# Prompt attention on one core: the values product of each head pair in eleven small groups instead of five

## What is computed

```python
k_nope = einsum('bsc,chd->bshd', c_kv, w_a_uk)
v = einsum('bsc,chd->bshd', c_kv, w_a_uv)
# for each block of 128 queries:
sc = (einsum('bqhd,bkhd->bhqk', qn_b, k_nope)
      + einsum('bqhd,bkd->bhqk', qr_b, k_r)) * ATTN_SCALE
sc = where(k_pos <= q_pos, sc, -inf)          # causal
p = softmax(sc, axis=-1)
o = einsum('bhqk,bkhd->bqhd', p, v)           # 16 heads, 64 values each
```

## Time and profile before

| | |
|---|---|
| median of 3 runs | 1721.11 us (1720.89 to 1722.8) |
| profiled execution | 1720.89 us, its span in the trace 1719.1 us |
| PE busy over the span | 1622.7 us (94%), 10281 matmuls |
| DVE busy | 950.2 us (55%) |
| ACT busy | 570.0 us (33%) |
| POOL busy | 200.1 us (12%) |
| `attend`, 136 to 521 us | PE busy 374.57 of 385 us at a granted clock of 1.00 |

### The profile page before, as it was taken

One profiled execution on the slowest core, in us unless ns is written; L12 is line 12 of the kernel. 1 busy time (PEld: TensorE's weight loads), 2 busy tenths in 40 slices (PEclk: granted clock), 3 DMA queues, 4 the chain that ended last, 5 costly groups with the idle time before them and its releaser, 6 DMA issues. The chain is left out here.

```text
span 1719.1 us, 29475 instructions
## 1 busy us (share of the span) xinstructions
PE 1622.7 (94%) x10281; PEld 1422.9 (83%) x10281; DVE 950.2 (55%) x1855; ACT 570.0 (33%) x1249; POOL 200.1 (12%) x292
## 2 busy tenths in 40 slices
PE   6989999999998999996997999999999999999995
PEld 6978888888885555554877999999999999999984
DVE  4556666656664445544554655456446554464469
ACT  4436555556552232323213311312212113122131
POOL 1000000000000000000341220211202202112001
PEclk9989999999998999996998999999999999999998
DMA  5211111011005656515102211101201111011003
GB/s 157 67 50 30 27 24 24 13 26 27 14 2 157 195 171 175 172 41 183 37 28 86 62 37 47 57 19 61 61 24 61 33 47 57 22 61 49 1 25 111
DMA packets 149343, 109.18 MB, mean 64 GB/s; under 512 B 54791, under 2 KB 137925, under 8 KB 149112
## 3 DMA queue, kind: packets, MB, share of 16 engines
q1 hardware_dynamic: 147848, 105.96, 21.3%
q0 software_dynamic: 816, 1.40, 0.4%
q10 hardware_dynamic: 576, 0.52, 0.1%
HBM read 101.88 MB, written 10.14 MB: 65 GB/s over the span
## 5 line engine op out<-in xcount | busy, mean ns | idle before, releaser
L1683 PE MATMUL banks<-act_hi,up_hi 128*128 128x352 f32 (+2 forms) x1056 | 341.8, 324 | 3.6 <-DVE up_lo L1921 3.6
L1684 PE MATMUL banks<-act_lo,up_hi 128*128 128x352 f32 (+2 forms) x1056 | 339.8, 322 | 0.0
L1685 PE MATMUL banks<-act_hi,up_lo 128*128 128x352 f32 (+2 forms) x1056 | 339.7, 322 | 0.0
L1683 PEld LDWEIGHTS banks<-act_hi,up_hi 128*128 128x128 f32 x1056 | 199.1, 189 | 3.7 <-ACT up_hi L1890 3.7
L1684 PEld LDWEIGHTS banks<-act_lo,up_hi 128*128 128x128 f32 x1056 | 199.3, 189 | 0.0
L1685 PEld LDWEIGHTS banks<-act_hi,up_lo 128*128 128x128 f32 x1056 | 199.0, 188 | 0.0
L1683 PE MATMUL banks<-gated_hi,down_hi 128*128 128x352 f32 (+2 forms) x528 | 172.0, 326 | 3.4 <-DVE o_t L2025 2.5
L1952 DVE TENSOR_TENSOR o_t<-o_t,banks 128x352 f32<-128x352 f32 x240 | 121.0, 520 | 93.8 <-PE banks L1685 93.5
L1931 DVE SCALAR_TENSOR_TENSOR conv_out<-conv_in,conv_now,conv_out 128x1072 f32<-128x1072 f32 x42 | 65.1, 1550 | 190.6 <-ACT conv_out L1831 190.6
L1684 PE MATMUL banks<-gated_lo,down_hi 128*128 128x352 f32 (+2 forms) x528 | 169.8, 322 | 0.0
L1685 PE MATMUL banks<-gated_hi,down_lo 128*128 128x352 f32 (+2 forms) x528 | 169.5, 321 | 0.0
(11 more groups left out here) (269 smaller groups left out, 3110.1 us busy)
## 6 DMA issues: line engine op xcount, KB each, us to landing
c_stage<-in_cache_kv_latent SPq DMA_DIRECT2D x252, 128.0 KB, 2.2
weight_stage<-in_w_f_up SPq DMA_DIRECT2D x44, 512.0 KB, 4.5
down_stage<-in_w_f_down SPq DMA_DIRECT2D x22, 512.0 KB, 4.3
o_t<-in_x_prompt SPq DMA_DIRECT2D x8, 512.0 KB, 3.8
rope_rows<-in_cache_k_rope SPq DMA_DIRECT2D x256, 16.0 KB, 2.0
r_stage<-rope_rows SPq DMA_DIRECT2D x16, 256.0 KB, 2.8
weight_stage<-in_w_a_out SPq DMA_DIRECT2D x8, 512.0 KB, 3.6
x_again<-in_x_prompt SPq DMA_DIRECT2D x8, 512.0 KB, 3.6
```

The source lines that it names most:

```text
L1683: nc.tensor.matmul(o, ws[0], xs[0], start=first, stop=False)
L1684: nc.tensor.matmul(o, ws[0], xs[1], start=False, stop=False)
L1685: return nc.tensor.matmul(o, ws[1], xs[0], start=False, stop=last)
```

## The change

Only the table changes. `VALUES_AT` gave the products of g = 3 to steps 5 and 7 (four blocks j each), those of g = 2 to 9 and 11 (three each), and those of g = 1 all to step 14 (four). Now g = 3 has steps 5, 6, 7, 8 with two blocks each, g = 2 has steps 9, 10, 11, 12 with 1, 2, 1, 2 blocks, and g = 1 has steps 13, 14, 15 with 2, 1, 1. The products of g = 0 stay behind the pair. No product is added or removed; a pair has 12 calls of `values` where it had 6. The orders of ACT, DVE, POOL and SP are the same as before.

```diff
-VALUES_AT = {5: (3, 0, 2), 7: (3, 2, 4), 9: (2, 0, 2), 11: (2, 2, 4), 14: (1, 0, 4)}
+VALUES_AT = {5: (3, 0, 1), 6: (3, 1, 2), 7: (3, 2, 3), 8: (3, 3, 4), 9: (2, 0, 1), 10: (2, 1, 2), 11: (2, 2, 3), 12: (2, 3, 4),
+             13: (1, 0, 2), 14: (1, 2, 3), 15: (1, 3, 4)}
```

## The result

The changed kernel takes 1736.58 us (median of 4 runs, 1735.02 to 1739.88) against 1721.92 us (4 runs, 1720.89 to 1722.8): a ratio of 1.0084, 95% interval 1.0067 to 1.0099. That is 14.7 us slower. The forecast was 7.8 us slower and its range ended at 1736, so the sign was right and the size was off by nearly a factor of two.

A forecast was written before the change was run, and what follows sets the result against it. PE bounds the attention (374.57 of 385 us busy). 1.08 + 0.25 - 0.05 - 0.21 = 1.07 us a pair, 7.5 for seven, plus 0.3 for the last: +7.8, forecast 1728.9 us; range 1722.5 to 1736.

The forecast's parts named there:

- the loss per group: Each new values group between transposes and a projection (steps 6, 8, 12) costs PE 0.36 us, 1.08 us a pair.
- the sign of being wrong: The prediction called itself wrong if a pair grew by less than 0.6 us or by more than 1.6.
- Step 10: New group between transposes and the inverse rows: a loss between 0.2 and 0.32 us, taken as 0.25.
- Step 13's stall: New group costs 0.25 us but outlasts a 0.30 us wait for the exponential of unit 13: net -0.05 a pair.
- Step 15: Last block of g = 1 behind k0: 0.57 us vanishes in PE's 0.88 us wait for scaled q00, -0.21 a pair.
- late next: At the pair's end, PE would still wait for the scaled q00, by some 0.3 us.
- The last pair: Without projections; six new groups, 1.8 to 2.2 us uncovered, shrink to +0.3 in total (between -0.3 and 1.5).
- Waits that move: DVE does not wait for g = 2; PE's bank 6 wait moves to step 13 with about 0.2 us margin.
- A: Rival: nothing is covered, every new group costs 0.36 us and stalls stay; 17.3 us slower, 1738; chance 0.08.
- B: Rival: the switch is free for small groups, only the covers count; -4 us, 1717; chance 0.06.
- C: Rival: loss half as large for small groups, 0.18 us; about 3 us slower in all, 1724; chance 0.12.
- D: Rival: the forecast plus a late bank 6 in step 13; +10 us, 1731; chance 0.06.

## Why the prediction was half right

- **The bound, and the loss per group: right.** PE's order decided. In the seven pairs a pair grew by 1.57 us, where 1.07 was forecast and 1.6 was the sign of being wrong. The loss of 0.36 us was measured as 0.34, 0.35 and 0.36 in steps 6, 8 and 12 (3 x 0.36 = 1.08, measured 1.05).
- **Step 10: 0.25 taken, 0.31 measured.** The rows gave 0.32 for the same passage; I had put part of it on the inverse rows without a row for that. Step 13 has the same error. Two times 0.06 over seven pairs is 0.8 us.
- **Step 13's stall: the step that failed.** The prediction took a stall of 0.30 us from the earlier trace rows and counted it for seven pairs, because "one (the fourth) stands for seven". It is there in the fourth pair alone: step 13 lasts 1.02 us in it and 0.67 in the six others. The same place of the next pair, kernel before:

```profile
372.73 0.38 PE L703 MATMUL banks<-ident,inv_rows 128*128 128x128 f32 x2
372.87 0.38 PE L580 MATMUL banks<-k_hi,q_hi 128*128 128x256 f32 x1
373.09 0.28 PE L581 MATMUL banks<-k_lo,q_hi 128*128 128x256 f32 x1
```

  0.14 us and no wait, against 0.49 (321.75 to 322.24). Of the six other pairs' -0.30 nothing was there to win: 1.8 us. In these six step 13 cost +0.31, not -0.05; in the fourth it came to -0.04. The list of waits could have warned: 6.1 us in 7 places proves only that the wait for q00 is in every pair. The stall starts on DVE, with the row maximum of unit 13, whose scores end with the mask product at 319.25 us in the fourth pair and 370.23 in the fifth:

```profile
319.92 0.42 DVE L871 TENSOR_REDUCE neg_max<-banks 128x1 f32<-128x256 f32 x1 [2.59 <-PE banks L657]
...
370.54 0.42 DVE L871 TENSOR_REDUCE neg_max<-banks 128x1 f32<-128x256 f32 x1 [2.24 <-PE banks L657]
```

  It starts 0.67 us after the mask product in the one and 0.31 in the other, with the same releaser, and the exponential behind it is as late. Why DVE is late in this one pair is open.
- **Step 15: right.** 0.57 us vanished in the 0.88, the wait is 0.29, and -0.24 was won where -0.21 was forecast.
- **The end of the pair: missed.** With the stall shorter, DVE's copy of the inverse sums falls on GpSimd's cast, 0.17 x 6 = 1.0 us. The prediction asked what is "late next" on the chain of q00 alone and not what runs beside the chain behind it.
- **The last pair: +0.3 forecast, +0.88 measured.** With g = 3 and g = 2 alone spread it was +0.17, so there the small stalls covered nearly all; what was missed is g = 1, whose spread adds 0.71.
- **Waits that move: right.** No wait for o_t in step 13; the run with g = 1 alone shows how near it was.
- **Rivals.** A (nothing is covered, 17.3 us) lay nearer to the total than the forecast did, though not to the attention's 11.35, and its mechanism is wrong: q00's wait did shrink. B and C fall by the table of steps, where groups of 4 to 8 records lose as much as those of 12 and 16. D's wait did not come up in this kernel.
- **Range.** The attention alone, 11.35 us, would have lain inside. The 3.3 us outside it, partly a slower stretch ahead of the attention that comes without the edit too and partly a longer mix, had no term at all; that the median came out at 1736.58, just above 1736, is as much theirs.

Sum of the misses in the attention: 0.8 + 1.8 + 1.0 + 0.6 = 4.2 us, less 0.2 each for the slightly smaller losses of steps 6, 8 and 12 and the larger gain of step 15, so 3.8, against 11.35 - 7.8 = 3.55. The steps rounded to 0.01 us make up the rest: they add up to 1.60 a pair, and 1.57 was measured.

## What to carry to other kernels

Products of 64 columns come in blocks: gather as many as the order allows, because each passage from 128-column work and back costs PE about 0.35 us that no busy time shows; read it from start to start. Put such a block where PE stands and not evenly. And before a stall of one period is multiplied by the number of periods, look it up in a second one.

## What the runs showed of the hardware

- Two fp32 products with 64 columns of weights, for the lower and the upper 64 partitions, run beside each other: a record of 256 columns takes 0.107 us (0.86 us for the 8 that left step 9), and 0.20 to 0.21 if both go to the lower half or have 128 columns.
- Entering a group of such products leaves the weight load idle for 0.17 us on average (6.6 us in 39 places), and the load after it for up to 0.4 us, without a semaphore. With twelve, six or four groups a pair the attention took 398.55, 387.2 and 382.2 us.
- A DVE copy from SBUF to SBUF (64 columns of fp32, 0.20 us) that starts during GpSimd's cast of 768 columns ends with it, after 0.74 us. The Trainium skill, page "SBUF — State Buffer", section "SBUF: two separate sides", has the port pair of the two as an exclusive lock for whole instructions, and the trace agrees in the main: the ends lie 0.05 us apart, and spans on GpSimd are rough. In the kernel before, a copy that overlapped the cast's last 0.09 us kept its 0.20. DVE's copy of the probabilities out of PSUM kept its length beside the next cast (0.41 us at 339.90).
